# A two-block transformer on one core: state outputs moved ahead of a column block, activation halves at other addresses, and the norm between the blocks without GpSimd

## What is computed

```python
for l in range(DEPTH):                       # first block, DEPTH = 2
    h = layer_norm(ALPHA * h + 0.5 * swiglu(h, gate, up, down), ln1_g[l], ln1_b[l])
    z, xbc, dt, fq, fk, fv, f, cq, ckv, kr = split(h @ w_in[l])
    y_ssd = ssd_mixer(...)   # y = scan + d_skip * xs; y = y * silu(z); rms_norm in 2 groups * norm_g
    mix = concatenate([y_ssd, fox_mixer(...), mla_mixer(...)]) @ w_out[l]
    h = layer_norm(ALPHA * h + mix, ln2_g[l], ln2_b[l])
    h = layer_norm(ALPHA * h + 0.5 * swiglu(h, ...), ln3_g[l], ln3_b[l])
x = h[:, N_META:]
for l in range(DEPTH):                       # second block
    h = rmsnorm(x, ffn1_norm[l]);  x = x + 0.5 * swiglu_2(h, ...)
    ...                                      # mixer, then a second feed-forward
return rmsnorm(x, final_norm)
```

## Time and profile before

| | us |
|---|---|
| median of 3 runs | 2091.39 (2091.3 to 2092.73) |
| the profiled execution | 2093.03 |
| its span, first to last instruction | 2091.1 |
| TensorE (PE) busy | 2035.1 |
| VectorE (DVE) busy | 1373.6 |
| ScalarE (ACT) busy | 974.5 |
| GpSimd (POOL) busy | 173.0 |

### The profile page before, as it was taken

One profiled execution on the slowest core, in us unless ns is written; L12 is line 12 of the kernel. 1 busy time (PEld: TensorE's weight loads), 2 busy tenths in 40 slices (PEclk: granted clock), 3 DMA queues, 4 the chain that ended last, 5 costly groups with the idle time before them and its releaser, 6 DMA issues.

```text
span 2091.1 us, 42117 instructions
## 1 busy us (share of the span) xinstructions
PE 2035.1 (97%) x16224; PEld 1978.7 (95%) x16224; DVE 1373.6 (66%) x2425; ACT 974.5 (47%) x1413; POOL 173.0 (8%) x215
## 2 busy tenths in 40 slices
PE   8999998999999999999997999999999999999998
PEld 8999888999999998799997999989999999989998
DVE  6774776775577657767745774667765775567765
ACT  4443764433443347544435444555444443455444
POOL 0000301200130012040003000000000000000000
PEclk9999999999999999999999999999999999999999
DMA  6454222445354533235554455335554555334553
GB/s 246 179 192 165 107 97 87 178 163 206 118 190 164 200 122 122 83 140 182 195 186 162 181 196 186 141 122 177 184 206 166 181 188 194 141 121 174 186 201 143
DMA packets 44508, 343.60 MB, mean 164 GB/s; under 512 B 4864, under 2 KB 5888, under 8 KB 6272
## 3 DMA queue, kind: packets, MB, share of 16 engines
q1 hardware_dynamic: 43536, 335.63, 44.6%
q0 software_dynamic: 880, 6.69, 0.9%
HBM read 341.25 MB, written 1.05 MB: 164 GB/s over the span
## 4 chain that ended last, share of the span: by engine, by line
PE 91%; DVE 4%; ACT 2%; issue 1%; POOL 0%; DVEq 0%; DMA 0%; ACTq 0%; POOLq 0%; SPq 0%
PE ps L507 29%; PE ps L509 28%; PE ps L508 28%; DVE w_lo L1563 1%; ACT w_hi L1079 1%; ACT x_hi L1130 1%; PE ps L763 0%; PE ps L754 0%; PE ps L711 0%; PE ps L943 0%; DVE x_lo L1619 0%; DMA h<-in_hidden 0%; PE ps L885 0%; PE ps L980 0%; DVE h L1631 0%
## 5 line engine op out<-in xcount | busy, mean ns | idle before, releaser
L507 PE MATMUL ps<-x_hi,w_lo 128*128 128x256 f32 (+3 forms) x3520 | 1025.5, 291 | 40.6 <-DVE x_lo L1619 20.6
L508 PE MATMUL ps<-x_lo,w_hi 128*128 128x256 f32 (+3 forms) x3520 | 1014.3, 288 | 0.0
L509 PE MATMUL ps<-x_hi,w_hi 128*128 128x256 f32 (+3 forms) x3520 | 1014.1, 288 | 0.0
L1563 DVE TENSOR_TENSOR w_lo<-raw,w_hi 128x1024 fp32r<-128x1024 f32 (+1 forms) x588 | 755.0, 1319 | 161.5 <-ACT w_hi L1079 160.7
L1079 ACT ACTIVATE w_hi<-raw 128x1024 fp32r<-128x1024 f32 (+1 forms) x588 | 634.4, 1119 | 298.3 <-PE ps L509 288.0
L507 PEld LDWEIGHTS ps<-x_hi,w_lo 128*128 128x128 f32 x3520 | 678.2, 193 | 53.4 <-issue 35.8
L508 PEld LDWEIGHTS ps<-x_lo,w_hi 128*128 128x128 f32 x3520 | 678.1, 193 | 0.8
L509 PEld LDWEIGHTS ps<-x_hi,w_hi 128*128 128x128 f32 x3520 | 678.1, 193 | 0.0
L507 PE MATMUL ps<-hid_hi,w_lo 128*128 128x256 f32 (+1 forms) x1536 | 434.6, 283 | 2.6 <-DVE hid_lo L2033 1.1
L509 PE MATMUL ps<-hid_hi,w_hi 128*128 128x256 f32 (+1 forms) x1536 | 436.2, 284 | 0.0
L508 PE MATMUL ps<-hid_lo,w_hi 128*128 128x256 f32 (+1 forms) x1536 | 432.1, 281 | 0.0
(11 more groups left out here) (236 smaller groups left out, 1157.1 us busy)
## 6 DMA issues: line engine op xcount, KB each, us to landing
raw<-in_w_up SPq DMA_DIRECT2D x178, 1024.0 KB, 4.8
raw<-in_w_down SPq DMA_DIRECT2D x64, 1408.0 KB, 6.0
raw<-in_w_in SPq DMA_DIRECT2D x36, 1024.0 KB, 4.8
raw<-in_w_out SPq DMA_DIRECT2D x16, 1024.0 KB, 4.8
cst<-in_consts POOLq DMA_DIRECT2D x1, 1664.0 KB, 6.6
cst<-in_consts POOLq DMA_DIRECT2D x1, 1537.5 KB, 6.7
prm<-in_prm POOLq DMA_DIRECT2D x2, 690.0 KB, 7.2
h<-in_hidden SPq DMA_DIRECT2D x1, 1088.0 KB, 7.0
```

The source lines that it names most:

```text
L507: mm(dst, w_lo[:, j, cols], xa, start=first, stop=False)
L508: mm(dst, w_hi[:, j, cols], xb, start=False, stop=False)
L509: return mm(dst, w_hi[:, j, cols], xa, start=False, stop=last)
L1563: v.tensor_tensor(w_lo[:, j, c], raw[:, j, c], w_hi[:, j, c].bitcast(F32), ALU.subtract)\
```

## The change

Three things. (1) Unused tiles of 64, 384 and 64 bytes are put ahead of `x_hi`, between it and `x_lo`, and behind `x_lo`, so that the halves start at 192 and 64 bytes modulo 512. (2) In `mixer1` all four `ssd_y` come before `block(19)`, `ssd_sums` right behind it; the banks they use change, DVE does four skips, the two normalisations and four gates together, ACT squares before `bias(19)`. The last attention pair goes to slot 7 of `x`, the state chunks to slots 3 to 6, with the rows of `w_out` in the new order. (3) The last layer norm of block one has its own form (`closing_norm`): no halves for it; DVE centres all chunks, then multiplies each by `rstd`; gain and bias are applied by DVE for even chunks and by ACT for odd ones; then come `x_hi`, square and `x_lo`. PE adds each square by a matmul of its own between the chunks of the first pair (`first_square`, `last_squares`). GpSimd does nothing of it, and its DMAs of constants wait for the squares.

```diff
         w_lo = sb("w_lo", [P, 2, 2 * W_WIDE], F32R)
+        sb("gap0", [P, 16])
         x_hi_all = sb("x_hi", [P, KD * X_PITCH], F32R)
+        sb("gap1", [P, 96])
         x_lo_all = sb("x_lo", [P, KD * X_PITCH], F32R)
+        sb("gap2", [P, 16])
...
-        Y_BANK, YSS_BANK, X_BANK, V_BANK, O_BANK = (3, 4, 2, 0), (5, 6), (5, 6, 7), 7, (7, 7, 7, 1)
-        SSD_SLOT = PAIRS
+        Y_BANK, YSS_BANK, X_BANK, V_BANK, O_BANK = (3, 4, 2, 5), (0, 2), (5, 6, 7), 7, (7, 7, 7, 1)
+        O_SLOT, SSD_SLOT = (0, 1, 2, 7), 3
...
+            def first_square(k):
+                pe.wait_ge(rms_sq, k + 1)
+                last = mm(ps[:, 7, 0:T2], con("onesD"), pj[:, KD + k, 0:T2], start=k == 0, stop=k == KD - 1)
+                if k == KD - 1:
+                    last.then_inc(var_ready, 1)
+            def last_squares():
+                for k in range(KD - 2, KD):
+                    first_square(k)
...
# ssd_y and ssd_sums on PE
-                    if c >= 2:
-                        pe.wait_ge(proj_scaled.sem, proj_scaled.at(l, 16 + c))
+                    if c == 2:
+                        pe.wait_ge(proj_scaled.sem, proj_scaled.at(l, 18))
+                    if c == 3:
+                        pe.wait_ge(pt_ready.sem, pt_ready.at(l, 3))
                     pe.wait_ge(sqy_ready.sem, sqy_ready.at(l, 1))
-                    pe.wait_ge(pt_ready.sem, pt_ready.at(l, PAIRS))
+                    pe.wait_ge(proj_scaled.sem, proj_scaled.at(l, 19))
+                    pe.wait_ge(y_taken.sem, y_taken.at(l, 4))
# the end of mixer1 on PE
                 att_o(2)
-                ssd_y(0)
-                ssd_y(1)
+                for c in range(4):
+                    ssd_y(c)
                 block(19)
+                ssd_sums()
                 att_t(3)
                 fox_values(1)
-                ssd_y(2)
-                ssd_y(3)
-                pe.wait_ge(y_taken.sem, y_taken.at(l, 2))
-                return {2: lambda: att_o(3), 3: ssd_sums}
+                return {3: lambda: att_o(3)}
# PE ahead of block two
+                if l == 0:
+                    up(q, t0 + SEC2["ffn1"], e0, T2, last_squares,
+                       {k + 2: lambda k=k: first_square(k) for k in range(KD - 2)})
# ACT
+            def closing_norm(norm, next_turn):
+                for k in range(KD):
+                    act.wait_ge(centered, norm * KD + (k + 1))
+                    fn(pj[:, KD + k, 0:T2], h[:, k, T1 - T2:T1], ACT.Square).then_inc(ln_sq, 1)
+                act.nop().then_inc(xh_ready, KD)
+                root(norm, T2, "eps1")
+                for k in range(KD):
+                    if k % 2 == 0:
+                        act.wait_ge(offset_v, k // 2 + 1)
+                    else:
+                        act.wait_ge(normed, k + 1)
+                        fn(h[:, k, T1 - T2:T1], h[:, k, T1 - T2:T1], ACT.Identity, scale=par(P1, "ln3g", k),
+                           bias=par(P1, "ln3b", k))
+                        act.drain()
+                    high(P1, "firstg", k, T2, T2)
+                    fn(pj[:, KD + k, 0:T2], h[:, k, T1 - T2:T1], ACT.Square).then_inc(rms_sq, 1)
+                second_pair(next_turn, 1)
...
                 gates()
+                ssd_squares()
                 bias(19)
                 o_high(0)
                 o_high(1)
+                ssd_rstd()
                 pt_copy(3)
                 o_high(2)
+                ssd_high(0)
+                ssd_high(1)
                 weights(22)
-                ssd_squares()
+                ssd_high(2)
+                ssd_high(3)
                 o_high(3)
-                ssd_rstd()
                 weights(23)
-                for c in range(4):
-                    ssd_high(c)
# DVE
+            def closing_norm(norm, next_turn):
+                def normalise(k):
+                    c = h[:, k, T1 - T2:T1]
+                    v.tensor_tensor(c, c, rstd[:, 0:T2], ALU.mult).then_inc(normed, 1)
+                    if k % 2 == 0:
+                        dve.drain()
+                        v.tensor_scalar(c, c, par(P1, "ln3g", k), par(P1, "ln3b", k), ALU.mult, ALU.add).then_inc(offset_v, 1)
+                dve.nop().then_inc(x_ready, KD)
+                dve.wait_ge(mean_ready, norm + 1)
+                for k in range(KD):
+                    v.tensor_tensor(h[:, k, T1 - T2:T1], h[:, k, T1 - T2:T1], ps[:, 6, 0:T2], ALU.subtract)\
+                        .then_inc(centered, 1)
+                dve.drain()
+                root(norm)
+                normalise(0)
+                normalise(1)
+                for k in range(KD):
+                    low(3 * DEPTH, P1, "firstg", k, T2, T2)
+                    if k + 2 < KD:
+                        normalise(k + 2)
+                lo_unit(next_turn, 1, 1, W_NARROW)
...
                 output(2)
-                skip(0)
-                skip(1)
+                for c in range(4):
+                    skip(c)
                 normalise(6)
                 normalise(7)
+                for c in range(4):
+                    gate(c)
                 scale(19)
-                gate(0)
-                gate(1)
                 o_low(0)
                 o_low(1)
                 fox_values(1)
-                skip(2)
-                o_low(2)
-                skip(3)
-                gate(2)
-                gate(3)
-                weights(22)
-                o_low(3)
                 dve.wait_ge(yrstd_ready.sem, yrstd_ready.at(l, 1))
                 for c in range(4):
                     ssd_norm(c)
+                o_low(2)
+                ssd_low(0)
+                ssd_low(1)
+                weights(22)
+                ssd_low(2)
+                ssd_low(3)
+                o_low(3)
                 weights(23)
-                for c in range(4):
-                    ssd_low(c)
...
# GpSimd
                 if l < DEPTH - 1:
                     layer_norm_sums(l * 3 + 2, T)
-                residual(l, 2, "ln3g", "ln3b", T)
+                    residual(l, 2, "ln3g", "ln3b", T)
                 pool.drain()
-            rms_norm_sums(0)
+            pool.wait_ge(rms_sq, KD)
```

More of the change, by code:

```diff
@@ L280, in build @@
         std_ready = sem("std_ready")
+        normed = sem("normed")
+        offset_v = sem("offset_v")
         out_ready = sem("out_ready")
@@ L533, in first_pair, with up @@
                             last.then_inc(unit_used, 1)
-            def up(q, turn0, event, T, after_first):
+            def up(q, turn0, event, T, after_first, before={}):
                 pe.wait_ge(up_free, q * NF + (CREDIT - 1))
-                first_pair(turn0, event, 0, T)
+                first_pair(turn0, event, 0, T, None, before)
                 after_first()
@@ L576, in rms_mean_square @@
             def rms_mean_square(norm):
-                mean_square(norm + 3 * DEPTH, rms_sq, norm * KD + KD, T2)
+                mean_square(norm + (3 * DEPTH - 1), rms_sq, norm * KD + KD, T2)
+            def first_square(k):
[6 more added lines that the diff above has]
+                    first_square(k)
             def down(q, turn0, resid, T):
@@ L1058, in _ @@
                 t0, q, e0, r0 = l * TURNS2 + BLOCK2_TURN, l * 2 + 2 * DEPTH, l * 4 + EVENT2, l * 3 + 3 * DEPTH
-                up(q, t0 + SEC2["ffn1"], e0, T2, lambda: rms_mean_square(l * 3))
+                if l == 0:
+                    up(q, t0 + SEC2["ffn1"], e0, T2, last_squares,
+                       {k + 2: lambda k=k: first_square(k) for k in range(KD - 2)})
+                else:
+                    up(q, t0 + SEC2["ffn1"], e0, T2, lambda: rms_mean_square(l * 3))
                 down(q, t0 + SEC2["ffn1"] + UP_T, r0, T2)
@@ L1284, in o_high @@
                     src = cqn[:, pair, T1 - T:T1] if pair < 3 else ps[:, O_BANK[pair], T1 - T:T1]
-                    fn(x_hi[:, pair, 0:T], src, ACT.Copy).then_inc(cat_hi.sem, 1)
+                    fn(x_hi[:, O_SLOT[pair], 0:T], src, ACT.Copy).then_inc(cat_hi.sem, 1)
                 def ssd_squares():
@@ L1523, in _ @@
                 down(t0 + SEC1["ffn2"] + UP_T, r0 + 2, False, r0 + 2, T)
[L1524 to L1529, removed]
+                if l < DEPTH - 1:
+                    layer_norm(r0 + 2, "ln3g", "ln3b", t0 + TURNS1, T)
+                else:
+                    closing_norm(r0 + 2, t0 + TURNS1)
             root(3 * DEPTH, T2, "eps2")
@@ L1845, in o_low @@
                 def o_low(pair):
-                    dve.wait_ge(cat_hi.sem, cat_hi.at(l, pair + 1))
-                    T = OUT_T[l]
+                    dve.wait_ge(cat_hi.sem, cat_hi.at(l, O_SLOT[pair] + 1))
+                    T, k = OUT_T[l], O_SLOT[pair]
                     src = cqn[:, pair, T1 - T:T1] if pair < 3 else ps[:, O_BANK[pair], T1 - T:T1]
-                    v.tensor_tensor(x_lo[:, pair, 0:T], src,
-                                    x_hi[:, pair, 0:T].bitcast(F32), ALU.subtract).then_inc(x_ready, 1)
+                    v.tensor_tensor(x_lo[:, k, 0:T], src,
```

(12 more changed lines are left out.)

## The result

The changed kernel takes 2063.09 us (median of 4 runs, 2062.48 to 2063.98) against 2091.35, a ratio of 0.9864 with a 95% interval of 0.9847 to 0.9881: 28.3 us faster, where 22.7 were forecast. The profiled execution took 2062.7 with a span of 2061.0, 30.1 less than the span of before.

What follows compares the result with a forecast made beforehand. TensorE was taken as the bound, busy 2035.1 of 2091.1 us. Savings of 11.0, 1.6, 3.6 and 6.5 sum to 22.7 us, from 2091.4 to 2068.7; own range 2062 to 2075, wide range 2056 to 2081.

Steps and rivals of the forecast that it cites:

- Addresses in block two: Block two's up- and input projections: 4992 matmuls reading `x` run 2.2 ns faster each, at `hid`'s rate; 11.0 us saved.
- Addresses in block one: Block one's matmuls of 274, 258 and 272 columns: 0.3 ns less for each of 5376; 1.6 us saved.
- The bounds of 16 us either way: Block one's odd lengths, 274 and 258 columns: from a fall to 11.0 ns beyond their columns' time to an equal rise.
- the rival in which the odd lengths fall too: Block one's 274 and 258 columns fall to 11.0 ns beyond their columns' time: 16.3 us instead of 1.6, 2054.0; chance 0.10.
- The rule of the Trainium skill: Start addresses change nothing for TensorE, so only the mixer and closing norm changes save: 10.1 us, 2081.3; chance 0.11.
- State outputs: End of block one's mixers, `ssd_y` before block 19: 1.8 us saved per layer, twice, 3.6 us; bounds 0 and 7.
- The new wait before the sums: Block one's mixer: PE idle from 316.6 to 319.1 before `ssd_sums`, until ACT's squares end; 2.5 us.
- The half clock of 3.4 us: Block one's mixer: 3.4 us at half clock after the new wait, costing 1.7 us.
- The second wait: Output projection after block one's mixer: PE idle 0.5 us more before the third chunk, `o_low(2)`, there at 324.9.
- The norm between the blocks: Block one's last layer norm without GpSimd: unit 2 starts at 1127.5 instead of 1134.0, 6.5 us saved; bounds 4.8 and 8.2.

## Why the prediction held, and where it was off

The wide range held the time and the sign was right; 22.7 us were forecast and 28.3 came. The forecast's own range, 2062 to 2075, held it at its edge; block one came out just above the 0 to 5 us that it allowed, at 5.3 to 6.0. By its steps:

- **Addresses in block two, 11.0 forecast, 13.9 in the trace.** The step that took the rate of `hid` for that of `x` at the same starts was right in kind (119.95 to 117.8 in one stage of four). Its size was short in the others: they ran at 117.0, and three hidden stages with them. Why the same loop body at the same addresses holds 117.0 in one layer and 117.8 in the next is open.
- **Addresses in block one, 1.6 forecast.** This is the term that was mis-sized most. I took the 0.3 ns of the row with 272 columns for the odd lengths, as the nearest. 272 columns gained nothing; 274 gained 1.5 and 2.3 ns, 258 gained 1.0. For 1056 matmuls each this is 1.6, 2.4 and 1.1 us, and about 0.9 ns for the 960 in the input projections 0.9: 6.0 us. About 0.7 of it belongs to the profile of before: in the five other traces with weights and `x` at one start, the stage from 590 us ran 0.7 ns faster than there. The bounds of 16 us either way held it; the rival in which the odd lengths fall too was right in part, by about a third of its 16.3 us. The tiles alone gave 18.1 us, where 12.6 were forecast for both address terms together.
- **The rule of the Trainium skill** ("SBUF — State Buffer", "SBUF: two separate sides") by which TensorE never waits on anyone on its side of the SBUF was a rival at 2081.3. The page says this of waits between engines; that start addresses would then change nothing was my reading. The runs decide against this reading: with nothing but 512 unused bytes placed, the kernel is 18.1 us faster. The prediction had no cause for the rate of `hid`, only the same starts. That 192 and 64 were chosen was no merit: each of the other three layouts with at least one half off the weights' start gave block two's `x` 117.8 ns or less too.
- **State outputs, 3.6 forecast, 3.9 measured alone.** The new wait before the sums was forecast at 2.5 us and is 2.4 (2.7 from start to start). The half clock of 3.4 us came in layer 0, where the sums took 3.5 us in place of 1.85, and not in layer 1; so the changed kernel's trace has 1.7 us for the one and 3.6 for the other, some 0.4 and 0.6 of them from the faster pitch. The second wait was 1.2 us where I had 0.5, and 1.3 in layer 1 at full clock, so the clock is not its reason. The schedule left out the two copies of `fox_values(1)`, which stand on DVE ahead of the norms: they waited for PE until 324.9, and the norms began 0.7 us after the root was there. The first pair ended at 333.9, where 331.0 + 1.7 = 332.7 was worked out; the other 0.4 of the difference were there before the sums, which began at 319.5 in place of 319.1.

```profile
324.92 0.42 DVE L1877 COPY scratch<-ps 128x256 f32<-128x256 f32 x1 [3.95 <-PE ps L749]
...
325.46 1.72 DVE L1924 SCALAR_TENSOR_TENSOR pj<-scratch,prm,std 128x272 f32<-128x272 f32 x4
```

- **The norm between the blocks, 6.5 forecast; 6.7 in the trace, 7.8 measured alone** (interval 4.8 to 9.8). PE started 8.6 us after the last mean matmul, where the schedule had 8.1; 3.4 us at half clock followed, as taken.
- **The clock.** Four layer norms lost their 3.4 us at half clock in this profile, which could pass for a gain of 1.7 each. It is not: among the 274-column up-projections with weights and `x` at one start, those with such a stretch took 139.9 to 140.0 us (139.7 without) in layer 0 and 139.7 to 139.8 (139.2 without, one trace) in layer 1; the 140.5 of before, at its slower pitch, is left out. What is lost comes back behind it, because there PE goes at the pace at which `x` is fed: in layer 1, the last chunks of the first pair took 0.77 us each behind such a stretch and 0.93 without.

## What to carry to other kernels

In a kernel bound by matmuls, look early at the starts of the operands, weights against moving halves, modulo 512 and modulo 256 bytes: a few hundred unused bytes were worth 0.9% here. A trace often holds the rate of another placement already, in a stage that reads another tile; take it as a lead, and then change one placement at a time to learn what it is that counts. When a step is moved up to hide a wait, write out who is late next: the first new wait here was read rightly from the durations of before, the second came out too short because one piece of DVE's list was left out, and filling both gave 8.2 us more than the changed kernel.

## What the runs showed of the hardware

- Matmuls of fp32r operands with 256 columns and chunks 1024 bytes apart ran at 120.0 ns when weights and both moving halves started at one address modulo 512 (all at 128 or all at 192), and at 116.7 to 117.8, in some stages 113.4, in the four other layouts; with 274 columns, 129.2 to 130.1 against 126.6 to 127.8. 192 and 448 gave the counts of 192 and 192.
- The same code at the same addresses holds one of several rates through a whole stage: 117.8, 117.0 and, twice with both halves at 192 and once with 192 and 448, 113.4 to 113.5 ns. For a stage of 1056 matmuls, 117.8 to 113.4 is 4.6 us. What picks the rate stays open; no run here sets it.
- 3.4 us at half clock cost 0.2 to 0.6 us after a layer norm, and about 1.7 in layer 0's mixer, where the sums took 3.5 us in place of 1.85.
